# Moving the SBUF start addresses of a two-block transformer kernel's tiles

## The reference, cut to what matters

```
h = rms_norm(x, w);  proj = h @ w_in                     # 2048 x 6160
x = x + concat(attention, gated_linear_attention) @ w_out
u = conv(rms_norm(x, w) @ w_up)                          # 2048 x 11264
x = x + (gelu(u_gate) * u_val) @ w_down                  # 5632 x 2048
x = x + sigmoid(rms_norm(x, w) @ w_ple_gate) * (p @ w_ple_proj)
...                                                      # second block: 2048 x 8704,
                                                         # two attention branches, swiglu
```

## Time and profile before

| | us |
|---|---|
| median of 3 runs | 2804.95 (2804.36 to 2805.76) |
| span of the profiled execution, first to last instruction | 2804.8 |
| TensorE busy in it | 2745.0 (98%) |
| TensorE weight loads | 2237.4 |
| VectorE busy | 1462.6 (52%) |
| ScalarE busy | 1333.0 (48%) |
| mean granted TensorE clock | 0.969 |

### The profile page before, as it was taken

How to read it: one execution, slowest core, us unless ns; L and a number is a source line. 1 busy time by engine, 2 the same in 40 slices (tenths; PEclk the granted TensorE clock), 3 DMA queues, 4 the chain that set the end, 5 groups by cost and what they waited for, 6 DMA issues and landing times.

```text
span 2804.8 us, 35705 instructions
## 1 busy us (share of the span) xinstructions
PE 2745.0 (98%) x12225; PEld 2237.4 (80%) x12225; DVE 1462.6 (52%) x1670; ACT 1333.0 (48%) x1675; POOL 18.3 (1%) x40
## 2 busy tenths in 40 slices
PE   8999989999999999999999999999999999999998
PEld 6888668888888888878788887778888888888886
DVE  5554445666666654455644445346554545454443
ACT  5333434656665643345533444464365444444333
POOL 1000000000000000000000000000000000000000
PEclk9999679999999999999999999599999999999999
DMA  8665115566666655565566664015566666666554
GB/s 269 191 193 167 43 35 185 173 194 181 189 186 186 186 187 189 188 192 188 170 189 187 187 187 150 1 41 191 181 180 188 192 188 189 188 188 203 188 188 139
DMA packets 246518, 479.40 MB, mean 171 GB/s; under 512 B 14708, under 2 KB 14820, under 8 KB 246176
## 3 DMA queue, kind: packets, MB, share of 16 engines
q1 hardware_dynamic: 244992, 471.97, 55.3%
q0 software_dynamic: 1440, 6.25, 0.6%
HBM read 476.06 MB, written 2.10 MB: 170 GB/s over the span
## 4 chain that ended last, share of the span: by engine, by line
PE 96%; DVE 2%; ACT 1%; issue 0%; DMA 0%; SPq 0%; ACTq 0%; DVEq 0%
PE acc L461 29%; PE acc L463 29%; PE acc L462 29%; PE acc L550 2%; PE tp L486 1%; PE tp L534 1%; PE tp L533 1%; PE tp L710 1%; PE tp L541 1%; DVE WL L1251 0%; PE tp L790 0%; PE tp L808 0%; PE tp L589 0%; PE tp L860 0%; DMA X<-in_x_dram 0%
## 5 line engine op out<-in xcount | busy, mean ns | idle before, releaser
L1251 DVE TENSOR_TENSOR WL<-WR,WH 128x1024 fp32r<-128x1024 f32 x892 | 1090.2, 1225 | 1145.3 <-ACT WH L898 1144.8
L898 ACT ACTIVATE WH<-WR 128x1024 fp32r<-128x1024 f32 x892 | 943.5, 1060 | 1265.2 <-PE acc L463 1248.7
L461 PE MATMUL acc<-WH,AH 128*128 128x512 f32 x2048 | 803.9, 393 | 0.0
L463 PE MATMUL acc<-WH,AL 128*128 128x512 f32 x2048 | 798.0, 390 | 0.0
L462 PE MATMUL acc<-WL,AH 128*128 128x512 f32 x2048 | 797.5, 389 | 0.0
L463 PEld LDWEIGHTS acc<-WH,AL 128*128 128x128 f32 x2048 | 384.6, 188 | 80.8
L461 PEld LDWEIGHTS acc<-WH,AH 128*128 128x128 f32 x2048 | 385.0, 188 | 78.8 <-issue 1.1
L462 PEld LDWEIGHTS acc<-WL,AH 128*128 128x128 f32 x2048 | 385.0, 188 | 78.1
L461 PE MATMUL acc<-WH,BH 128*128 128x512 f32 x704 | 279.0, 396 | 0.0
L463 PE MATMUL acc<-WH,BL 128*128 128x512 f32 x704 | 278.4, 395 | 0.0
L462 PE MATMUL acc<-WL,BH 128*128 128x512 f32 x704 | 278.4, 395 | 0.0
(11 more groups left out here) (266 smaller groups left out, 1797.7 us busy)
## 6 DMA issues: line engine op xcount, KB each, us to landing
WR<-in_w_in_dram SPq DMA_DIRECT2D x232, 512.0 KB, 4.3
WR<-in_w_ffn_up_dram SPq DMA_DIRECT2D x176, 512.0 KB, 3.7
WR<-in_w_ffn_down_dram SPq DMA_DIRECT2D x176, 512.0 KB, 4.5
WR<-in_w_ffn_in_dram SPq DMA_DIRECT2D x176, 512.0 KB, 3.7
WR<-in_w_out_dram SPq DMA_DIRECT2D x64, 512.0 KB, 3.8
WR<-in_w_ple_gate_dram SPq DMA_DIRECT2D x32, 512.0 KB, 4.5
WR<-in_w_branch_a_dram SPq DMA_DIRECT2D x16, 512.0 KB, 3.7
WR<-in_w_branch_b_dram SPq DMA_DIRECT2D x16, 512.0 KB, 4.2
```

The costliest lines, as they stand in the source:

```text
L461: pe.matmul(o, H[:, kt + k, cols], WH[:, s, k], start=begin, stop=False)
L463: mm = pe.matmul(o, L[:, kt + k, cols], WH[:, s, k], start=False, stop=end)
L898: act.activation(WH[:, n % RING], WR[:, n % RING], ACT.Copy).then_inc(hi_done, 1)
L1251: dve.tensor_tensor(WL[:, n % RING], WR[:, n % RING], WH[:, n % RING].bitcast(F32), ALU.subtract).then_inc(lo_done, 1)
```

## The change

`vec`, `ss` and `ssum` move to the front, and then `place` is rounded up to a multiple of 2,048; `junk` moves in front of the constants; `base` is rounded up to a multiple of 512. No instruction, wait, loop, size or queue is changed.

```
@@ -146,6 +146,12 @@
 
         ends = []
 
+        vec = sb("vec", [P, 6 * KT + 4 * 2 * FKT])
+        ss = sb("ss", [P, TB, 4])
+        ssum = sb("ssum", [P, TB])
+        nw = vec[:, 0:6 * KT].rearrange("p (n k) -> p n k", k=KT)
+        cw = vec[:, 6 * KT:].rearrange("p (n k) -> p n k", k=2 * FKT)
+        place[0] += -place[0] % 2048
         X = sb("X", [P, TB, D])
         stationary = place[0]
         AH = sb("AH", [P, KT, T], F32R)
@@ -153,22 +159,18 @@
         WR = sb("WR", [P, RING, CHUNK_KT, NT])
         WH = sb("WH", [P, RING, CHUNK_KT, NT], F32R)
         WL = sb("WL", [P, RING, CHUNK_KT, NT], F32R)
+        junk = sb("junk", [P, NT])
         ident = sb("ident", [P, P])
         tri_le = sb("tri_le", [P, P])
         tri_gt = sb("tri_gt", [P, P])
         neg_tri = sb("neg_tri", [P, P])
         neg_ones = sb("neg_ones", [P, P])
         neg_mask = sb("neg_mask", [P, P])
-        vec = sb("vec", [P, 6 * KT + 4 * 2 * FKT])
-        nw = vec[:, 0:6 * KT].rearrange("p (n k) -> p n k", k=KT)
-        cw = vec[:, 6 * KT:].rearrange("p (n k) -> p n k", k=2 * FKT)
-        junk = sb("junk", [P, NT])
-        ss = sb("ss", [P, TB, 4])
-        ssum = sb("ssum", [P, TB])
         smean = sb("smean", [P, TB])
         sroot = sb("sroot", [P, TB])
         inv = sb("inv", [P, 7, TB])
-        base = place[0]
+        base = place[0] + (-place[0]) % 512
+        assert stationary % 2048 == 0 and base % 512 == 0
```

More of the change, by code:

```diff
@@ L161, in two_blocks_kernel @@
         neg_mask = sb("neg_mask", [P, P])
[L162 to L167, removed]
         smean = sb("smean", [P, TB])
```

## The result

The changed kernel takes 2778.77 us (median of 4, 2777.89 to 2780.06) against 2805.02 us (4 runs): a ratio of 0.9906, with a 95% interval of 0.9894 to 0.9918. It is 26 us faster, where 148 us were forecast. The time is just inside the upper end of the range, 2,780 us, and far from the forecast of 2,657. The spans of the profiled executions go from 2804.8 to 2778.3 us, 26.5 us less.

What follows compares the result with a forecast made beforehand. TensorE's product stream was taken as the bound; 70.0 us from A and 82.1 us from B, together 152 us, less 4 us not gained, gave 148 us off 2,804.8, so 2,657 us, with a range of 2,630 to 2,780 us at 0.81.

Steps and rivals of the forecast that it cites:

- What bounds the kernel: TensorE's own stream, busy 98% of the span and 96% of the chain; its fp32r products take 2,457 of 2,804.8 us.
- Where the surplus comes from: Time per product over 213.3 ns was blamed on operand start addresses off multiples of 512, likely gone at offset 0.
- A: The 6,144 products with stationary operand in front of `base` (`AH`/`AL`), 226.7 ns each; 13.3 ns blamed on offset 128.
- B: The 4,560 products with stationary operand behind `base`, 233.3 ns each; the further 6.7 ns blamed on stationary offset 192.
- The reading of the earlier trace that cleared the weight load: A product with no weight load behind it for 4 us also took 0.39 us, so the load costs no 13.3 ns.
- The main term: Products fall to 215.3 ns: A gains 70.0 us, B 82.1 us, together 152 us; chance 0.62.
- The gate rows: Gate products of 256 columns average 118.1 ns, 11.5 over, at all stationary offsets; each should lose some 10 ns.
- Only `base` counts: Rival: 13.3 ns belong to fp32r, only B falls to 226.7 ns; 30 us gained, 2,774.5 us; chance 0.19.
- Slower: Rival: moving and stationary reads collide at equal offsets, A rises by 6.6 ns, 41 us lost, 2,846 us; chance 0.08.
- Nothing changes: Rival: SBUF reads have no grain wider than 64 bytes, so no address gains or loses; 2,805 us; chance 0.11.
- What else is touched: VectorE and ScalarE passes keep 1,225 and 1,060 ns, covered by TensorE; waits and half-clock products cost 4 us of the gain.
- the ring: Slots for loaded weights keep up: landing, `hi` and `lo` make 6.8 us against 10.3 us for four chunks.

Runs made afterwards that it cites:

- the bfloat16 run: The changed kernel with `WH` and `WL` written as bfloat16 side by side, stationary pieces read as the upper two bytes of each float32: 2659.14 us.

## Why the prediction was wrong, point by point

- *What bounds the kernel* was right: TensorE's stream, 96% of the chain before and after, and the intervals of 226.7 and 233.3 ns.
- *Where the surplus comes from* failed. The step that failed was "What all of these share is a moving operand that begins 128 bytes past a multiple of 512", with "the two surpluses equal the larger offset of each kind, to the column" as its main reason. All fp32r products of the kernel before had the same moving offset, so nothing in its trace could show that the offset mattered; that 32 and 48 columns match 128 and 192 bytes was chance. What the runs showed in its place: moving offsets of 0, 64 and 128 all give 226.7 ns when the distance is 0, so A's 13.3 ns are not a matter of the start address, and B's further 6.7 ns hang on the distance of 64 between its two operands. The reading of the earlier trace rows that cleared the weight load carried nothing: the end of a product is modelled, so its 0.39 us say nothing of the load.
- *The main term* was wrong with it: 11.4 ns × 6,144 for A came out as 0, and 18.0 ns for B as 6.7.
- The gate rows were read by their mean alone, and so as "not by the stationary address". Taken one by one, their 47 intervals in the trace of the kernel before run from 112 to 123 ns (but for the first), and the sequence repeats to the nanosecond after 24 products, which are eight steps of 64 bytes. In the changed kernel the same sequence comes three products, one step, later, to 1 ns once it has settled, as the distance is 64 bytes less there. So the trace of before did show an effect of the distance, which the mean hides: a walk through all distances has the same mean wherever it starts. That is why these products still take 118 ns.
- *Only `base` counts*, at 0.19, had the right sum, 30 us off and 2,774.5 us against 2,778.8 measured, and the right intervals, A at 226.7 and B falling to it. Its reason was wrong: rounding `base` alone brings 0.8 ns of the 6.7. The sum is right only because the front moved as well, which took the distance to 0. That the measured time lies within the stated range is owed to this rival, which the range was stretched to hold, and not to the mechanism that I forecast.
- *Slower* had the collision of moving row and stationary piece in view, and dismissed it since A was the quicker. A was quicker because it was at distance 0; I took equal residues for the worst case where they are among the best. The case that "A is the quicker one, which is against it" was the key to the result, read the wrong way round.
- *Nothing changes* rested on the 16-byte lines of the Trainium skill ("SBUF — State Buffer", specifications). A grain of 16 bytes fits part of what the runs show: 16 away from 0 costs nothing or (240, second block) 1.7 ns, while 4 and 8 cost 4 to 5 ns. But among multiples of 32, all on such lines, there are differences of 6.7 ns, which the page doesn't have.
- What else is touched: VectorE's 1,225 and ScalarE's 1,060 ns, and the ring, stood as said. The rings' spare time could be seen in the bfloat16 run, where an interval of 216 ns ran through.

## What to carry to other kernels

For fp32r products, lay moving rows and stationary pieces so that their start addresses are the same modulo 256 (modulo 512 is what the quickest kernels have); the absolute alignment is of no account here, and 64 bytes between them cost 6.7 ns on top of 226.6 in every product of 512 columns at the full clock. When two groups of one instruction run at different speeds, list all that differs between them before extrapolating either: a property that all of them share explains nothing. Look at single intervals as well as at their mean. And two points lie on a line with anything; a cheap kernel that shifts one tile by 64 bytes says more.

## What the runs showed of the hardware that I had not expected

- The interval of an fp32r product of 512 columns depends on the distance of its two operands' addresses, from 226.6 to some 234 ns, and not smoothly: 192 gives 228.9 between 233.3 at 160 and 233.4 at 224. The pattern comes back after 256 bytes in three pairs of four; with 256 columns, in the gate stage, it comes back after 512.
- The Trainium skill says that loading the next weights doesn't take reading bandwidth from the running product ("TensorE: Matmul & The Clock Gate", on LDWEIGHTS), and that on the engines' side of SBUF only a port pair shared by two other engines makes for contention ("SBUF — State Buffer", "Who interferes with whom"). The distance effect speaks against that for 4-byte operands: the distance of two addresses that TensorE reads decides 6.7 ns, with VectorE and ScalarE at rest as well. That it is the weight load that meets the stream is my reading, not shown.
- With 64 or 32 stationary columns an fp32r product takes 230 to 232 ns, more than the 226.6 with 128.
- 512 columns of two-byte operands take 225.1 ns at a step of two and 215.9 with the moving ones side by side.
